# Ranking all keys of the second token block first, and moving 26 row products of 32 tokens into the first expert table's last chunks

## What is computed

```python
q = (xt @ w_pq).reshape(t, PK_HEADS, 2, PK_DQ // 2)            # 8 heads
scores = jnp.einsum('thpc,hpnc->thpn', q, sub_keys)            # 2 x 128 keys a head
s1, i1 = lax.top_k(scores[:, :, 0], 16); s2, i2 = lax.top_k(scores[:, :, 1], 16)
cand_s = s1[..., :, None] + s2[..., None, :]                   # 256 candidates
top_s, sel = lax.top_k(cand_s, 16); idx = ...                  # 16 of 16384 experts a head
gates = jax.nn.softmax(top_s, axis=-1)
pre = jnp.einsum('tkd,td->tk', expert_u[idx], x)               # 8 * 16 = 128 experts a token
act = jax.nn.gelu(pre) * gates
out = jnp.einsum('tk,tkd->td', act, expert_v[idx])
```

## Time and profile before

| | |
|---|---|
| median of 3 runs | 2092.58 us |
| lowest, highest | 2089.2, 2094.84 us |
| the profiled execution | 2100.03 us, its span 2098.2 us |
| mean granted TensorE clock in it | 0.991 of full speed |

### The profile page before, as it was taken

The page is one execution under the profiler, slowest core; times in us unless marked ns, Lnnn a source line. Parts: engine busy times, 40 slices in busy tenths (PEclk is TensorE's granted clock), DMA queues, the critical chain, the costliest instruction groups (busy, mean ns, idle before and its releaser), DMA issues.

```text
span 2098.2 us, 38198 instructions
## 1 busy us (share of the span) xinstructions
PE 2038.6 (97%) x12234; PEld 1862.9 (89%) x12234; DVE 1636.4 (78%) x2521; ACT 1079.5 (51%) x1452; POOL 716.6 (34%) x422
## 2 busy tenths in 40 slices
PE   8999999979999999999999999999999999999997
PEld 7888778978789999999999999989999899999885
DVE  6885777974667888888888657888888788888765
ACT  6543566334435745554555444555555555555554
POOL 0030200000002888887888850322322323344000
PEclk9999999989999999999999999999999999999998
DMA  5755558225555878887778877999999899999554
GB/s 202 256 180 180 171 171 305 96 88 193 201 171 180 212 210 208 205 210 209 209 207 208 221 239 243 327 333 343 342 336 328 285 306 331 359 343 330 193 187 141
DMA packets 171797, 496.14 MB, mean 236 GB/s; under 512 B 48689, under 2 KB 48977, under 8 KB 169809
## 3 DMA queue, kind: packets, MB, share of 16 engines
q1 hardware_dynamic: 117056, 413.39, 59.7%
q0 software_dynamic: 51200, 67.25, 12.2%
q10 hardware_dynamic: 3472, 14.72, 1.9%
HBM read 476.24 MB, written 19.04 MB: 236 GB/s over the span
## 4 chain that ended last, share of the span: by engine, by line
PE 75%; DMA 11%; DVE 8%; ACT 2%; issue 2%; DVEq 1%; SPq 0%; ACTq 0%
PE ps L262 27%; PE ps L267 15%; PE ps L1962 10%; DMA raw<-in_v_table 9%; PE ps L1967 5%; PE ps L288 5%; PE ps L282 5%; PE ps L283 5%; DVE lo L242 3%; ACT hi L236 2%; DMA arena<-in_u_table,few_pick 1%; PE ps L1847 1%; DVE act_pair L373 1%; DVE arena L1493 1%; PE ps L1857 0%
## 5 line engine op out<-in xcount | busy, mean ns | idle before, releaser
L236 ACT ACTIVATE hi<-raw 128x1024 fp32r<-128x1024 f32 x724 | 767.7, 1061 | 875.1 <-PE ps L262 387.0
L242 DVE TENSOR_TENSOR lo<-raw,hi 128x1024 fp32r<-128x1024 f32 x724 | 891.8, 1235 | 351.3 <-ACT hi L236 327.2
L1679 POOL DMA_INDIRECT gate_map<-gate_in_sb x256 | 473.6, 1850 | 540.1 <-DVEq L1443 464.6
L262 PE MATMUL ps<-act_pair,hi 128*128 128x448 f32 (+1 forms) x2816 | 655.5, 374 | 0.9 <-ACT hi L236 0.5
L262 PEld LDWEIGHTS ps<-act_pair,hi 128*128 128x128 f32 x2816 | 504.5, 189 | 51.9 <-DVE act_pair L373 1.8
L267 PEld LDWEIGHTS ps<-act_pair,lo 128*128 128x128 f32 x2816 | 372.0, 191 | 18.2 <-DVE lo L242 3.1
L267 PE MATMUL ps<-act_pair,lo 128*128 128x224 f32 (+1 forms) x2816 | 375.3, 276 | 1.4 <-DVE lo L242 1.4
L1962 PE MATMUL ps<-stage,hi 128*128 128x448 f32 x1024 | 233.0, 369 | 7.8 <-ACT hi L236 5.9
L1962 PE MATMUL ps<-act_pair,hi 128*128 128x448 f32 x1024 | 230.2, 367 | 1.6 <-ACT hi L236 1.3
L1696 POOL DMA_INDIRECT arena<-in_u_table,few_pick x64 | 97.9, 1530 | 322.4 <-DVE keep L1493 288.1
L1962 PEld LDWEIGHTS ps<-stage,hi 128*128 128x128 f32 x1024 | 183.5, 189 | 23.5 <-issue 7.5
(11 more groups left out here) (269 smaller groups left out, 1652.5 us busy)
## 6 DMA issues: line engine op xcount, KB each, us to landing
raw<-in_expert_u SPq DMA_DIRECT2D x256, 512.0 KB, 3.7
raw<-in_v_table SPq DMA_DIRECT2D x256, 512.0 KB, 7.1
raw<-in_w_in_cols SPq DMA_DIRECT2D x64, 512.0 KB, 3.3
raw<-in_w_in_rows SPq DMA_DIRECT2D x48, 512.0 KB, 3.2
raw<-in_w_out SPq DMA_DIRECT2D x32, 512.0 KB, 3.4
raw<-in_w_pq SPq DMA_DIRECT2D x32, 512.0 KB, 3.2
raw<-in_w_gate SPq DMA_DIRECT2D x32, 512.0 KB, 4.1
gate_map<-stage SPq DMA_DIRECT2D x1, 14336.0 KB, 41.5
```

Source lines behind the costliest of these rows:

```text
L236: act.activation(hi[:, use, :], raw[:, slot, :], ACT.Copy).then_inc(hi_ready, 1)
L242: dve.tensor_tensor(lo[:, use, :], raw[:, slot, :], hi[:, use, :].bitcast(F32), ALU.subtract).then_inc(lo_ready, 1)
L262: mm = pe.matmul(first_tokens(out_ap), hi[:, use, d8 * P:(d8 + 1) * P], first_tokens(act_pair[:, d, :]), start=(d == 0), stop=False)
L1679: pool.indirect_dma_start(gate_map, bass.IndirectOffsetOnAxis(ap=place[0:n, unit, r:r + 1], axis=0), gates_out[0:n, unit, r:r + 1], None, ...
```

## The change

1. Scores are stored with the second token block ahead of the first (`scores_block`), so units 0 to 7 are heads of the second block and units 8 to 15 of the first (`block_of`).
2. The picks of the 32 tokens are then known after the fourth weighing. `few_ids` runs there; their DMAs are issued in the fifth and sixth weighing, and `few_norm` (two multiplies 128x1024) runs after the sixth. `few_weight` is a new place for the norm's weights.
3. GpSimd issues the first 16 U fetches between the 32 scatters of the eighth weighing, one after every two scatters. A unit's scatters now wait for those of the unit directly before it, when both are of one block.
4. 26 of the 64 U products run at the end of chunks 102 to 127 of the U stage, one to a chunk. The other 38 are spread over V steps 2 to 97, and the V products over steps 102 to 253. The first 18 V fetches use two slots, later ones four. The gelu of the 32 tokens moves from the second half of the V stage to its 25th round.
5. The sum of a chunk's two PSUM halves is split: ScalarE copies one half from PSUM to `pre` (`copy_pre`), and VectorE adds the other half (`take_pre`).

```diff
+FEW_KNOWN = PK_HEADS // WEIGH_UNITS - 1
+FEW_KNOWN_ROUND = 25
+DOTS_FROM = LAST_WEIGH // 2 + 2
+EARLY_DOTS = 26
+TWO_SLOTS = 18
...
+        def block_of(unit):
+            return TB - 1 - unit // PK_HEADS
...
+            def copy_pre(c, parity):
+                act.wait_ge(expert_bank, c + 1)
+                act.wait_ge(lo_used, T_U + 2 * c + 2)
+                act.activation(pre[:, parity], ps[:, U_BANK + parity, SEQ:SEQ + MANY], ACT.Copy).then_inc(pre_copied, 1)
...
             def take_pre(c, parity):
-                dve.wait_ge(lo_used, T_U + 2 * c + 2)
-                dve.wait_ge(expert_bank, c + 1)
-                dve.tensor_reduce(pre[:, parity, :], both_halves(U_BANK + parity)[:, 0:MANY, :], AX_X,
+                dve.wait_ge(pre_copied, c + 1)
+                dve.tensor_tensor(pre[:, parity], ps[:, U_BANK + parity, 0:MANY], pre[:, parity],
                                   ALU.add).then_inc(pre_ready, 1)
...
+            for c in range(LAST_WEIGH // 2, CHUNKS):
+                for k in range(2):
+                    rest_tile(dve, *tile_at(T_U, c // 2, 4, 2 * (c % 2) + k)[:3])
+                take_pre(c - 1, (c - 1) % 2)
+                if DOTS_FROM <= c < DOTS_FROM + EARLY_DOTS:
+                    few_half(*halves_u[c - DOTS_FROM])
...
-            FEW_U_FROM, FEW_U_TO, FEW_V_FROM, FEW_V_TO = 2, 140, 147, 253
+            FEW_U_FROM, FEW_U_TO, FEW_V_FROM, FEW_V_TO = 2, 4 * FEW_KNOWN_ROUND - 3, 4 * FEW_KNOWN_ROUND + 2, 253
...
+            def fetch(n, q):
+                r, table = n % FEW_STEPS, u_table if n < FEW_STEPS else v_table
+                slot, _ = few_slot(n, q)
+                k = 2 * (n - FEW_STEPS) + q - TWO_SLOTS
+                if k >= FEW_SLOTS:
+                    pool.wait_ge(few_done, 2 * n + q - FEW_SLOTS + 1)
+                elif k >= 2:
+                    pool.wait_ge(stage_lo_ready, CHUNKS + 14)
+                elif n >= 1:
+                    pool.wait_ge(few_done, 2 * n + q - 1)
...
             for w in range(WEIGHINGS):
                 pool.wait_ge(gates_ready, w + 1)
                 for unit in range(WEIGH_UNITS * w, WEIGH_UNITS * (w + 1)):
-                    if unit >= TB:
-                        pool.wait_ge(gates_placed[unit % TB], 16 * TOPK * (unit // TB))
+                    b, before = block_of(unit), unit % PK_HEADS
+                    if before > 0:
+                        pool.wait_ge(gates_placed[b], 16 * TOPK * before)
                     for r in range(TOPK):
-                        n = P if unit % TB == 0 else FEW_FROM
+                        n = P if b == 0 else FEW_FROM
...
+                        if w == WEIGHINGS - 1 and r % 2 == 1:
+                            k = TOPK * (unit % WEIGH_UNITS) + r
+                            if k == 1:
+                                pool.wait_ge(few_read, 16 * FEW_GROUPS)
+                            fetch(*fetches[k // 2])
+            for n, q in fetches[TOPK * WEIGH_UNITS // 2:]:
+                fetch(n, q)
```

More of the change, by code:

```diff
@@ L826, in expert_round @@
                         round_tile(act, *tile_at(T_U, i, 4, 2 * c + k))
+                    if not (first and c == 0):
+                        copy_pre(2 * i + c - 1, 1 - c)
                     if not first:
@@ L859, in _ @@
-            act.wait_ge(few_written, 16 * 2)
-            for g in range(FEW_GROUPS):
-                at = slice(g * FEW, (g + 1) * FEW)
-                picks = slice(g * FEW_STEPS, (g + 1) * FEW_STEPS)
-                act.dma_start(few_pick[at], few_picks.rearrange("s q h r -> s q (h r)")[:, :, picks]).then_inc(few_read, 16)
-                if g % 2 == 1:
-                    expert_round(FEW_ROUND + 6 + g // 2)
-            with act.Fori(FEW_ROUND + 8, CHUNKS // 2) as i:
+            with act.Fori(LAST_WEIGH // 4, CHUNKS // 2) as i:
@@ L878, in value_round @@
                     round_tile(act, T_V + v, c % RAW, c % SPLIT, T_V // RAW + CHUNKS // RAW * half + i)
+                    if first and c == 0:
+                        copy_pre(CHUNKS - 1, 1)
                     if first and c < 2:
@@ L1422, in weigh @@
                 dve.tensor_tensor(gates3[:, units], best_all[:, units], top_first, ALU.subtract).then_inc(gates_in, 1)
-                for tb in range(TB):
-                    dve.tensor_scalar(place_f[:, tb::TB], picks_all[:, 1, units][:, tb::TB], float(MANY),
-                                      keep[:, C_TOKEN + tb:C_TOKEN + tb + 1], ALU.mult, ALU.add)
+                token = C_TOKEN + block_of(WEIGH_UNITS * w)
+                dve.tensor_scalar(place_f, picks_all[:, 1, units], float(MANY), keep[:, token:token + 1], ALU.mult, ALU.add)
                 dve.drain()
@@ L1510, in few_weigh @@
                 dve.drain()
-            halves_u = [(n, q) for n in range(FEW_STEPS) for q in range(2)]
             halves_v = [(n, q) for n in range(FEW_STEPS, 2 * FEW_STEPS) for q in range(2)]
@@ L1671, in _ @@
             pool.wait_ge(map_cleared, 16)
+            def fetch(n, q):
[8 more added lines that the diff above has]
+                    pool.wait_ge(few_done, 2 * n + q - 1)
+                pool.indirect_dma_start(few_slots[slot], None, table.rearrange("e (h f) -> (e h) f", h=2),
+                                        bass.IndirectOffsetOnAxis(ap=few_index[:, q, r:r + 1], axis=0)
+                                        ).then_inc(few_landed[slot], 16)
+            fetches = [(n, q) for n in range(2 * FEW_STEPS) for q in range(2)]
             for w in range(WEIGHINGS):
```

134 lines of the change are left out of this document (69 added, 65 removed).

## The result

The changed kernel takes **2144.39 us** (median of 4 runs, 2143.35 to 2144.83) against 2093.71 us of the kernel before on the same chip (4 runs, 2089.2 to 2095.45). The ratio is 1.0236, 95% interval 1.0221 to 1.0251: slower by 50.7 us. The forecast was 2103.3 us with a range up to 2118. The direction was right, the size was not.

What follows compares the result with a forecast made beforehand. TensorE was taken as the bound, with V losing time to transfers. U loss +20.6, seam +0.3 and V gain -10.2 gave +10.7 us on the median 2092.6: 2103.3 us, 8-in-10 range 2084 to 2118.

Steps and rivals of the forecast that it cites:

- GpSimd's start of the eighth weighing: U stage: longer units and landing waits make GpSimd start these scatters 15 us late, at 1175.6; bounds 1 and 20.
- The first four weighings: GpSimd's scatters of 96-token units: 2 x 32.5 + 5.4 = 70.4 us a pair, even with the 70.66 us between weighings.
- The landing: Time from a GpSimd scatter's end until it has landed, which the next unit waits for: taken as 3.0 us.
- The split sums: U stage: VectorE's shorter add and ScalarE's PSUM copy, costed at nothing except 0.3 us at the change to V.
- The gain in the V stage: Fewer fetches beside V's tiles lower DMA demand: 10.2 us won, bounds 0 and 14.4.
- line from 334 to 350 GB/s: V stage: loss drawn from none at 334 GB/s of demand to 11.9 us at 350, leaving 3.2 us after the change.
- the slack: End of U: the first early product may start until 1177.0 us, the sixteenth until 1252.6, before TensorE waits.
- the pace of 5.6 us: GpSimd's eighth weighing: two scatters and a fetch take 5.6 us, one of three held, against a chunk's 5.04.
- the seam: Change from U to V stage: ScalarE's copy between TensorE's last product and the sum freeing the bank costs 0.3 us.
- a third hold in each chunk: U stage: early products with two SBUF inputs hold GpSimd, +0.15 us a step, 2 us in all beside the sum.
- GpSimd keeps up: Rival at the eighth weighing: U loses up to 3 us, V gives 10 to 12, time 2083.6 us; chance 0.18.
- GpSimd is held at every request: Rival: steps of 6.5 to 7 us, U loses 30 to 50 us, time some 2122 us; chance 0.08.

Runs made afterwards that it cites:

- e1: Changed kernel with odd units scattering into a second, unused map and each unit waiting only for the landing two units before: 2097.47 us, ratio 1.0011.
- e8: Changed kernel without its split sums: one VectorE reduction takes both PSUM halves and ScalarE copies nothing; 2133.81 us, ratio 1.0186.
- e4: Kernel before, with each unit's scatters waiting for the landing of the unit directly before instead of two before: 2093.44 us, ratio 0.9997.
- e9: Kernel before with the split sums and nothing else of the change: 2093.62 us, ratio 0.9996.
- e5: e1 with 24 of the 26 early fetches left out, the 26 products kept on whatever lies in their slots: 2091.85 us, ratio 0.999.
- e7: Kernel before, own order and unit waits, with 10 early products at chunks 117 to 126, 54 over V steps 2 to 140: 2090.44 us, ratio 0.9984.
- e6: e1 with 21 early products, one each 1.2 chunks, instead of 26 at one a chunk: 2093.8 us, ratio 0.9998.
- e2: Changed kernel without early products or fetches between scatters, leaving the ranking order and split sums: 2102.11 us, ratio 1.0039.
- e3: Changed kernel with 10 early products instead of 26, 1.6 chunks apart, one fetch after every third scatter: 2107.33 us, ratio 1.0054.

## Why the prediction was wrong

**GpSimd's start of the eighth weighing** is the step that failed: "I take 15 us late, bounds 1 and 20". It was 42 in the changed kernel. What the step had, and what the runs showed in its place:

- *The first four weighings.* The step called them even: "2 x 32.5 + 5.4 = 70.4" (waits of 3.0 us behind units of 32.47 give 70.9). They made GpSimd 23 us late (971.01 against 948.25), a mean unit of 38.2 us in place of 35.2. The 32.5 us were those of 96-token units in the second place of a weighing. The duration belonged to that place beside VectorE's work, not only to the number of tokens: in e1 a scatter of 96 tokens takes 1.89 us in the mean in the first unit of a weighing and 1.80 in the second. The 128 scatters of these weighings take 1.85 us in the mean, and 1.75 in the rows that the step went by, which is 13 us. In e8, without the split sums, GpSimd is 12.7 us late here, so 10 of the 23 come with them.
- *The landing.* 3.0 us were taken, 3.5 measured (48.6 us in 14 times), so 7 us over the way. The waits themselves are shown by e4, which adds them alone (25 us late), and by e1, where they are gone and the three pauses with them (2 us late). The Trainium skill (DMA: Bandwidth & Descriptors, section Anatomy of one DMA) puts the fixed time at about 2.0 us: the trace agrees only with the shortest, 2.13 us at 1202.58, when the queues were nearly empty.
- *The three pauses.* They are 10.9 us in all and have no counterpart in the step. Their cause stays open.
- *The split sums.* They were costed at nothing, and as work that holds (e9, e5). But with them scatters begin earlier inside the rests and take longer, which gives 10.7 of the 42 us (e8) and 10.6 to 13 us of the time. The step took GpSimd's holds as they were before.

These items overlap: the first holds shares of the others. Counted apart, from the first scatter to the eighth weighing's first (537.0 us, 493.9 in the kernel before), the 43 us are: 42.5 for 13 landing waits, 10.0 for the three pauses (both beyond the usual gap of 0.3), 11.5 for longer scatters, less 20.7 us of spare time ahead of the weighings, all of which is used up.

Carried on by the prediction's own sum, this explains the time: the scatters start 27 us later than the 1175.6 assumed; the sixteenth fetch is issued 93.3 us after them (91.1 forecast); it lands after 8.1 us (6.5 taken: product at 1304.04). That is 51.4 us after the limit of 1252.6, in place of 20.6. The U stage lost 54.4; the other 3 are about what TensorE's slower clock behind the stall cost (below).

**The gain in the V stage** was mis-sized: 10.2 us forecast, about 3 measured in medians (e5), and 4.4 from the result itself (54.4 + 0.7 - 50.7). The profiles of before and after show 10, since the one profile of before was of an execution 7.4 us above the median. Its V stage lost 14.0 us up to the second half. That of e4, with the same transfers, lost 6.7, and that of e9 2.3. The prediction subtracted the 7.4 us from the level but left them in the gain. The mechanism stands, by the two groups of profiles under e7: with 81 to 83 GB/s of fetches the first half runs at TensorE's pace, with 94 to 98 it loses 2.3 to 14.0 us. How much a kernel loses at the denser rate varies more from one execution to the next than the prediction's line from 334 to 350 GB/s allows.

**Right steps.** The place of the stall and its chain; the slack (product needed by 1177.0); the pace of 5.6 us (5.55 to 5.66 in e1; in the changed kernel 93.3 / 16 = 5.83 with one landing); the last ten early products lost 0.0 us; products, norm and sums are free as work; the seam cost 0.7 us in place of 0.3. The first 38 us of loss came from the first product, not from a slow growth to the sixteenth: 34.9 of TensorE's idle time are its lateness, and the pace adds the rest.

Products do hold GpSimd, as rests do. This is the second fetch of the changed kernel:

```profile
1211.33 1.43 POOL L1720 DMA_INDIRECT arena<-in_u_table,few_pick  x1 [0.30 <-issue]
```

It begins inside the first product (1210.66 to 1211.89) and ends 0.87 us behind its end; a free one takes 1.00. In e1 twelve scatters and fetches before 1310 us begin inside a product and take 4.3 us more than free ones in all, and in the changed kernel twelve take 4.0 us more. The Trainium skill (SBUF — State Buffer, section Who interferes with whom) says that a VectorE instruction with two SBUF inputs contends with a GpSimd instruction that reads SBUF, and these traces agree. The prediction counted the product by it as a third hold in each chunk, 2 us beside its sum. How often they meet is another matter. In e5, which has the products without the fetches, one scatter does: its unit beside the products takes 40.4 us with two fetches in it (1.67 and 1.01 us, with gaps), so 37.1 for the scatters, where the unit at this place took 38.1 before.

**The rivals.** "GpSimd keeps up" was tried in e1 and e6: even on time the time is 3 us longer (e1) or the same (e6), not 9 us shorter, since V has less to give. "GpSimd is held at every request" did not happen in the changed kernel, where VectorE's own waits freed it, but e2 and e3 show it in the unit ahead of the eighth weighing, 43 to 44.5 us with its landing: its scatters take 2.24 and 2.23 us in the mean, none under 2.2. Not tried was a kernel with the right result in the new order and with no landing wait, since each unit adds to the map that the unit before it adds to.

## What to carry to other kernels

- An engine that is "free 2.5 us before the next piece of work" has no slack for a wait of 3.5 us in each half of it; such a wait adds up over all repetitions before the place where it is needed. Sum it from the first repetition on, and take durations from each place beside the other engines' work.
- Before work is moved ahead of a due time, list all due times of the engine that must feed it. Here there were two, the first product and the gate blocks in SyncE's queue; the second one alone makes the new order cost 8 us.
- A gain that is read from one execution is only as good as that execution. Where it lies above the median, the surplus may be the very loss that the change is to win back. Ten products moved where the feeding engine was free, with the rest over the same steps as before, thinned V's transfers as much as 26 packed into fewer steps, which ended 50.7 us slower.

## What the runs showed of the hardware

- After 34.87 us without work TensorE ran its next matmuls at the lower of its two levels, 1.2 in place of 2.4 GHz: 3.21 us for eight of 448 columns against 1.80, and 2.05 against 1.05, for some 6 us, then at full rate. The granted clock of the window of the stall is 0.61. This cost 2 to 3 us. In e2, 8.63 us without work had the same effect: 3.19 us for eight of 448 columns.
- A scatter into HBM with add is held by a VectorE that works on two SBUF tensors. Of the 621 scatters in the kernel before, the changed kernel, e1 and e9 that begin inside a rest or a product, 620 end 1.25 to 1.5 us behind the end of it, however early they begin. They take 2.22 us at the usual place in a rest, and 1.55 to 1.57 us each, fourteen in a row, while VectorE waited. A stall on VectorE so shortens its own cause, by some 10 us here (lateness 42 against 50 and 54 in e3 and e2).
- The landing of such a scatter, from the end of its instruction on, took 2.1 to 4.4 us in the changed kernel, the least when the DMA share was 0.30, and 6.2 at most in e8.
- A cheaper instruction on VectorE (0.38 for 0.62 us), with a copy on ScalarE ahead of it, made GpSimd slower, by 0.11 us a scatter (e9): 59 in place of 30 scatters then begin in the first 0.4 us of a rest.
